# Three attention stages of an fp32 transformer kernel rewritten: dilated attention by query classes over 688 keys, weighted sums turned round

## The reference

```python
def neighbourhood_attention(q, k, v, rpb):      # each query: 8 rows x 16 columns of keys
    s = q.k * d ** -0.5 + bias;  pr = softmax(where(valid, s, NEG));  return pr @ v

DIL_CONFIGS = ((128, 1), (512, 4), (2048, 16))  # (window, dilation)
def dilated_branch(q, k, v, pos, slopes, window, dil):
    # query t attends to t + j*dil for |j| <= window // (2*dil)
    s = q.k * Dh ** -0.5 - slopes * abs(pos_q - pos_k)
    ...
def dilated_attention(...):                     # the three branches, weighted by their denominators
    return sum(outs * softmax(lses))

def latent_attention(...):                      # MLA: q and k of width 96 (64 + 32 rotated)
    s = (qn.kn + qr.kr) * scale;  p = softmax(s);  return p @ v
```

## Time and profile before

| what | value |
|---|---|
| median of 3 runs | 4692.28 us (4685.75 to 4693.0) |
| profiled execution, its own time | 4690.71 us |
| span of the profile | 4688.9 us |
| PE busy | 4082.2 us, 87% of the span |
| DVE, ACT, POOL busy | 48%, 32%, 37% |
| mean granted clock of PE | 0.948 of full speed |

### The profile page before, as it was taken

One profiled execution on the slowest core, in us unless ns is written; L12 is line 12 of the kernel. 1 busy time (PEld: TensorE's weight loads), 2 busy tenths in 40 slices (PEclk: granted clock), 3 DMA queues, 4 the chain that ended last, 5 costly groups with the idle time before them and its releaser, 6 DMA issues.

```text
span 4688.9 us, 60744 instructions
## 1 busy us (share of the span) xinstructions
PE 4082.2 (87%) x22152; PEld 3480.2 (74%) x22152; DVE 2228.0 (48%) x4269; ACT 1503.3 (32%) x2417; POOL 1736.7 (37%) x1140
## 2 busy tenths in 40 slices
PE   3999575788789798998899999688898996999998
PEld 2788465776577687886688888576887885888887
DVE  2443585532366565553444443465565544323323
ACT  2221243431233674441221211232773432222221
POOL 2432123531255462002544444353560003544442
PEclk9999888999899899998999999899999998999999
DMA  6765332631135422212223221245322221111111
GB/s 152 207 179 149 98 89 64 138 100 50 72 88 140 111 60 66 48 50 90 78 84 108 77 99 32 76 119 146 84 55 63 54 80 49 50 49 54 45 45 50
DMA packets 300704, 404.65 MB, mean 86 GB/s; under 512 B 45908, under 2 KB 224980, under 8 KB 299860
## 3 DMA queue, kind: packets, MB, share of 16 engines
q1 hardware_dynamic: 293496, 375.60, 28.5%
q10 hardware_dynamic: 6912, 25.17, 1.8%
HBM read 316.23 MB, written 93.63 MB: 87 GB/s over the span
## 4 chain that ended last, share of the span: by engine, by line
PE 68%; issue 8%; DVE 7%; POOL 5%; DMA 3%; SPq 2%; DVEq 2%; ACT 2%; POOLq 1%; ACTq 0%
PE ps L881 10%; PE ps L456 6%; PE ps L458 5%; PE ps L457 5%; PE ps L871 5%; PE ps L1834 5%; PE ps L1835 5%; PE ps L1836 5%; PE ps L1850 5%; PE ps L1852 4%; PE ps L1851 4%; POOL rs L770 2%; PE ps L917 1%; DVEq L1235 1%; PE ps L1507 1%
## 5 line engine op out<-in xcount | busy, mean ns | idle before, releaser
L405 POOL TENSOR_TENSOR WL<-RAW,WH 128x1024 fp32r<-128x1024 f32 x226 | 556.6, 2476 | 1195.1 <-ACT WH L387 1184.9
L456 PE MATMUL ps<-WH,XTh 128*128 128x512 f32 (+1 forms) x1536 | 616.9, 402 | 70.6 <-issue 34.8
L457 PE MATMUL ps<-WH,XTl 128*128 128x512 f32 (+1 forms) x1536 | 604.2, 393 | 0.0
L458 PE MATMUL ps<-WL,XTh 128*128 128x512 f32 (+1 forms) x1536 | 604.0, 393 | 0.0
L387 ACT ACTIVATE WH<-RAW 128x1024 fp32r<-128x1024 f32 x226 | 234.1, 1057 | 794.2 <-PE ps L1852 347.8
L1870 DVE TENSOR_TENSOR X<-ps,X 128x512 f32<-128x512 f32 x512 | 349.0, 689 | 254.1 <-PE ps L1852 253.1
L1850 PE MATMUL ps<-WH,Hh 128*128 128x512 f32 x1024 | 401.3, 392 | 4.3 <-DVE X L1870 4.0
L1834 PE MATMUL ps<-XTh,WH 128*128 128x512 f32 x1024 | 400.4, 391 | 1.2 <-issue 1.2
L1835 PE MATMUL ps<-XTl,WH 128*128 128x512 f32 x1024 | 398.9, 390 | 0.0
L1836 PE MATMUL ps<-XTh,WL 128*128 128x512 f32 x1024 | 398.8, 389 | 0.0
L1852 PE MATMUL ps<-WL,Hh 128*128 128x512 f32 x1024 | 398.6, 389 | 0.0
(11 more groups left out here) (196 smaller groups left out, 7664.0 us busy)
## 6 DMA issues: line engine op xcount, KB each, us to landing
RAW<-w_all SPq DMA_DIRECT2D x232, 512.0 KB, 4.0
WM<-w_mod ACTq DMA_DIRECT2D x48, 512.0 KB, 4.2
WM<-w_mod SPq DMA_DIRECT2D x48, 512.0 KB, 4.0
QS<-QA_d SPq DMA_DIRECT2D x24, 512.0 KB, 3.9
KHs<-KA_d SPq DMA_DIRECT2D x48, 256.0 KB, 6.0
KLs<-KA_d SPq DMA_DIRECT2D x48, 256.0 KB, 6.5
VS<-VA_d SPq DMA_DIRECT2D x20, 512.0 KB, 7.3
X<-x SPq DMA_DIRECT2D x2, 4096.0 KB, 12.8
```

The source lines that it names most:

```text
L405: e.tensor_tensor(w_low(n), w_raw(n), w_high(n).bitcast(F32), ALU.subtract).then_inc(w_ready, 1)
L456: e.matmul(bank, a, w, start=(kc == 0), stop=False)
L457: e.matmul(bank, b, w, start=False, stop=False)
L458: j = e.matmul(bank, a, l, start=False, stop=(kc == K - 1))
```

## The change

In all three stages the sum over the keys is turned round: the values are split into a high and a low fp32r part that stand side by side (64 + 64 columns, VHL) as the stationary operand, and the turned probabilities, also split into high (PTh, ACT) and low (PTl, DVE), are the moving one with 512 queries, for four units (a group G) at once. The 128 x 512 result is copied by ACT to OT, and PE turns it back and adds the two halves by four plain fp32 matmuls of 64 columns against twoI (two identities on top of each other). DVE divides and writes four tiles of Y at once. The negation of the maximum is folded in. The two halves of 4 heads are one run of 64 units.

Dilated attention takes as a unit not 128 neighbouring queries but one residue class mod 4 of 512 queries. Its keys are then 576 near ones and 112 far ones of the same class, 688 in place of 1024. A query's slope is folded into q (POOL multiplies the eps and sums of squares of a head by a table column, `by_head`), so that the bias ND is a table that stays and gets one addition of log counts per head. The output product's transposes put Y's dilated columns back in order of tokens (`by_class`, a write with a stride of 4).

NA and dilated attention ("narrow") share one body, `band_pe`, `band_act`, `band_dve`, and MLA has `heads_pe` and so on. In the narrow body the scores run two units ahead, probabilities have three buffers, the first four turned pieces go to bank 4 + u % 2 and the rest (one in NA, two in dilated) to bank 7, which is a single buffer; bank 6 holds the sum.

```diff
+        def band_pe(who, a):
+            def scores(u):
+                at = band(a, u)
...
+                if u >= 2:
+                    e.wait_ge(s["max"], a.u0 + min(u - 1, N_UNITS))
...
+                G = hosts_back(u)
+                if G is not None:
+                    e.wait_ge(s["ot_copied"], a.g0 + G + 1)
+                    for r in range(4):
+                        c = at.back + 64 * r
+                        j = e.matmul(flat(2 * (u % 2), c, c + 64), a.OT[:, G % 2, r * P:r * P + P], twoI[:], start=True, stop=True)
+                    j.then_inc(s["back"], 1)
...
+                for keys, c in at.keys:
+                    to = flat(2 * (u % 2), c, c + len(range(S)[keys]))
+                    e.matmul(to, Q[:, h % 2, at.queries], KH[:, h % 2, keys], start=True, stop=False)
+                    j = e.matmul(to, Q[:, h % 2, at.queries], KL[:, h % 2, keys], start=False, stop=True)
+                j.then_inc(s["full"], 1)
+            def turn_first(u):
+                e.wait_ge(s["exp"], a.u0 + u + 1)
+                ge(e, s["lo"], 2 * (a.u0 + u) - 3)
...
+            def turn_rest(u):
+                at = band(a, u)
+                ge(e, s["lo"], 2 * (a.u0 + u))
+                for src, c in at.rest:
+                    j = e.transpose(ps[0:src.stop - src.start, 7, c:c + P], Pt[:, u % 3, src], ident[:])
+                j.then_inc(s["tr"], 1)
...
+            scores(0)
+            scores(1)
+            for u in range(N_UNITS + 6):
+                G, r = divmod(u - 1, 4)
+                if u < N_UNITS:
+                    turn_first(u)
+                    turn_rest(u)
+                scores(u + 2)
+                if 1 <= G <= N_GROUPS and r < 3:
+                    values(G - 1, r)
...
+        def band_dve(who, a):
...
+            maxes(0)
+            for u in range(N_UNITS + 7):
+                if u + 1 < N_UNITS:
+                    maxes(u + 1)
+                if 1 <= u <= N_UNITS:
+                    low(u - 1)
+                if u % 4 == 2 and u >= 10:
+                    output(u // 4 - 2)
...
+        def heads_pe(who, a):
...
+            scores(0)
+            for u in range(N_UNITS + 4):
+                G, r = divmod(u, 4)
+                if u + 1 < N_UNITS:
+                    scores(u + 1)
+                if u < N_UNITS:
+                    turn(u)
+                if G >= 1 and r < 3:
+                    values(G - 1, r)
+                if G >= 1 and r == 3:
+                    turn_back(G - 1)
```

More of the change, by code:

```diff
@@ L814, in in_cell, with qk_kind @@
             return lambda kc: (first + kc // kper, (kc % kper) * width)
-        def qk_kind(dst, gain, first):
+        def qk_kind(dst, gain, first, by_head=False):
             def store(e, t, m, slot):
@@ new lines, in build_program, with __init__ @@
+        class Dilated:
+            def __init__(self, u):
+                g, c = divmod(u % T, 4)
+                self.g, self.first, self.width = g, 0, DIL_KEYS
+                self.queries = slice(512 * g + c, 512 * g + 512, 4)
+                if g == 0:
+                    far = slice(576 + c, S, 4)
+                    self.flat, self.nat, self.back = 0, 0, 768
+                    self.keys = [(slice(0, 512), 0), (slice(512, 576), 512), (far, 576)]
+                    self.rest = [(slice(512, 512 + DIL_FAR), 0), (slice(576, DIL_KEYS), P)]
+                    self.rest_rows = DIL_FAR
+                else:
+                    far = slice(c, 448, 4)
+                    self.flat, self.nat, self.back = S - DIL_KEYS, DIL_KEYS - 512, 512 - 512
+                    self.keys = [(far, 336), (slice(448, 512), 448), (slice(512, S), 512)]
+                    self.rest = [(slice(48, 48 + P), 0), (slice(0, P), P)]
+                    self.rest_rows = P
@@ new lines, in na_pool @@
+        def na_pool(who, a):
+            e, s = who.e, a.s
+            value_low(e, a, 0)
+            for u in range(N_UNITS):
+                h, t = divmod(u, T)
+                if t == 0:
+                    e.wait_ge(*a.loaded(h))
+                    nab = NAB[:, h % 2, :].rearrange("p (a b) -> p a b", b=GRID_W)
+                    e.tensor_tensor(nab, nab, rows3(CMK[:], NA_E, GRID_W), ALU.add)
+                    e.drain()
+                if u >= 3:
+                    e.wait_ge(s["max"], a.u0 + u - 2)
+                e0 = (NA_START[t] - 2 * t + 8) * GRID_W
+                e.tensor_tensor(BIn[:, u % 3, :], NAB[:, h % 2, e0:e0 + NA_KEYS], RMK[:, NA_KIND[t], :], ALU.add).then_inc(s["bias"], 1)
+                if u % T == 7 and u + 1 < N_UNITS:
+                    value_low(e, a, u // T + 1)
@@ new lines, in dil_attention @@
+                    g, c = divmod(t, 4)
+                    if g == 0:
+                        parts = [(slice(0, 576), slice(0, 576)), (slice(576, DIL_KEYS), slice(576 + c, S, 4))]
+                    else:
+                        parts = [(slice(0, DIL_FAR), slice(c, 448, 4)), (slice(DIL_FAR, DIL_KEYS), slice(448, S))]
+                    for cols, keys in parts:
+                        j = e.activation(ND[:, t, cols], POSF[:, keys], ACT.Abs, bias=rs1[:, t:t + 1])
+                    j.then_inc(s["dist"], 1)
@@ L1976, in layout @@
     out["pos_cols"] = v["positions_2"][0].reshape(T, P).T
+    out["pos_class"] = v["positions_2"][0].reshape(2, P, 4).transpose(1, 0, 2).reshape(P, T)
     out["w_mod"] = v["w_mod_2"]
```

719 lines of the change are left out of this document (458 added, 261 removed).

## The result

The changed kernel takes 4753.93 us (median of 4 runs, 4752.26 to 4755.9) against 4689.01 us for the kernel before (4 runs, 4684.69 to 4693.0): the ratio is 1.0139, 95% interval 1.0121 to 1.0156. The forecast was 4660, range 4605 to 4735: wrong in sign and outside the range. The profiled execution took 4752.26 us, its span 4750.4, 61.5 more than before.

The account below looks back on a forecast made before the run. PE was taken to bound dilated attention and MLA before, a loop of waits the narrow stages after; +23 (NA) + 0 (dilated) - 62 (MLA) + 3 (elsewhere) + 6 (clock) = -30 gave 4660 us, range 4605 to 4735.

Parts of the forecast that it names:

- The loop of waits: Narrow units: turned rest, scores, maximum and both low parts follow each other without overlap, once a unit.
- its sum: Loop terms added up: 3.80 us a dilated unit (3.73 before) and 3.33 us an NA unit.
- I take 0.107: PE, new small fp32r products: 0.107 us each, since each has one weight load; bounds 0.03 to 0.06 and 0.214.
- the second rival: Small products at plain fp32 pace, or slow strided reads: 0.43 us a dilated unit, 0.21 an NA unit; 4728 us; chance 0.15.
- one sentence: Query weights and keys read with stride 4: no row shows whether they cost more; the high bound covers it.
- I put 6 us for a few such stretches: Narrow stages: a few stretches at half clock, where the loop grows by 1.1 us, cost 6 us in all.
- the third rival: Narrow stages: clock falls to 0.88, half clock a quarter of the time, 0.28 us a unit; 4707 us; chance 0.14.
- PE's share of work: Argument against a falling clock: PE works 65 to 70% of the loop, a little above differential attention.
- the start and the tail of the stage: Dilated attention: first counted maximum about 3.5 us later than the old first one, tail 11 us; stage 246 us, no difference.
- NA: the number: NA stage 23 us slower: first maximum 6 us later, 210 us of units, tail 10.5, against 203 before.
- MLA: MLA units 3.50 us, 0.56 less, with a longer tail: 31 us gained a layer, 62 in all.
- Elsewhere: Other stages: `by_head` costs 3 us; strided writes by ACT and DVE nothing, at most 10.

Follow-up runs that it names:

- Experiment 2: Changed kernel with PE's turned rest moved behind the scores of unit u+2: 4540.22 us, ratio 0.9679 to the kernel before.
- Experiment 8: Changed kernel with contiguous dilated queries (other than the reference's) and three no-work products between PE's two turned parts: 4644.16 us, ratio 0.9904 to the kernel before.
- experiment 1: Changed kernel with dilated queries from 128 contiguous columns, so other queries than the reference's: 4696.6 us, ratio 1.0017 to the kernel before.
- experiment 4: Changed kernel with a filler, three small no-work products between PE's two turned parts in narrow units: 4722.1 us, ratio 1.0067 to the kernel before.
- experiment 7: Changed kernel with turned rest behind the scores and GpSimd copying each head's queries sorted by class: 4475.96 us, ratio 0.9546 to the kernel before.
- experiment 5: Changed kernel with turned rest behind the scores and contiguous dilated queries (other than the reference's): 4475.32 us, ratio 0.9546 to the kernel before.

## Why the prediction was wrong

- **The loop of waits: right in place and members, its sum partly by luck.** In the changed kernel DVE waited 322.5 us for PE's scores before its 128 dilated maxima, and PE waited before L1418 for DVE's low part (0.73 us in the row at 1707.98). Experiment 2 opens the loop by moving one of its members. Experiment 8's averages, 3.82 us (3.80) and 3.30 us (3.33), look like its sum measured, but each has a term too much and one too little. Dilated: turned rest 0.17 (0.21) and scores to maximum 1.19 to 1.22 (1.30) make a round of 3.66, and the filler and the start of the stage fill it up to 3.82. NA: turned rest to maximum is 1.00 (0.11 + 1.12), a unit without turn-backs 2.90 (3.12), and seven changes of head of 4.6 to 5.5 us, at which the sum had put nothing, bring the average back up.
- **"I take 0.107" for the small products: this term failed, in dilated attention.** It was right where queries are contiguous (0.11 in experiment 1, and in the changed kernel's own value products). Loads with a stride of 4 fp32 numbers follow each other after 0.22 to 0.23 us. It was the second rival, 0.15 with slow strided reads in it, whose price of 0.43 us a unit came out at 0.46 (experiment 1 against the changed kernel) and, at nearly full clock, 0.60 (experiment 4 against 8, 277.92 - 240.35 = 37.6 us for 63 units); its NA part did not come, as NA's queries have no stride. A row of before could not show it, and I let one sentence stand for a cost that the change adds to all six score products of a unit. The Trainium skill (SBUF — State Buffer, section Door 1: The DMA port swizzle) has the rule that I left out: SBUF is read in lines of 16 bytes, and an access that goes to a new line each time pays. A stride of 4 fp32 numbers is just 16 bytes. The trace agrees, 0.19 us for a contiguous load and 0.33 for a strided one. No run here has another stride, so it is not shown here that the line of 16 bytes is the reason.
- **"I put 6 us for a few such stretches" of lower clock: mis-sized.** It was the third rival in dilated attention: a granted clock of 0.76, lower than the 0.88 of differential attention that I took for the rival. Its price, 1.1 us a unit times 0.48, would be 0.53. The windows give 0.25 (experiment 4 against the changed kernel) to 0.39 (experiment 8 against 1); with the filler's own 0.50 us in every fourth unit taken out, 0.37 to 0.52. So the price was about right, and what failed was the choice of 6 us in its place. I had gone by PE's share of work, and this case's rows do not bear that out: PE was busy for 249 of 294 us in the dilated window at a clock of 0.76, for 164 of 214 in NA at 0.86, and for 83 of 120 in differential attention before at 0.88. What sets the clock stays open; the runs show that it rose when the pauses were filled (experiment 4) and when the loop was opened (experiment 2).
- **The two together** are 293.90 - 240.35 = 53.6 us from first to last maximum in layer 0 and 48.7 in layer 1, 102 of the 123 us of both layers. The other 10 us a layer lie in the start and the tail of the stage: in the changed kernel the first two units took 9.6 us, forecast 3.5, and 15.2 us lie behind the last maximum, forecast 11 (layer 0).
- **NA: the number right, in part by luck,** +25.0 against +23. The first maximum came 0.6 us later and not 6; the 63 units took 214.2 us against 210, with the low clock in them (experiment 4 gives 4.9 us less), and the tail 13.2 against 10.5.
- **MLA: right in mechanism, too small.** 3.38 us a unit ((2130.46 - 1917.46) / 63) against 3.50, and before 4.10 ((2086.64 - 1828.43) / 63) against the 4.06 of the one unit that I had read, since the average holds the pause between the two halves. After the change the four units of a group repeat as 3.66, 3.66, 3.17 and 3.16 us, each some 0.1 under its forecast. The stage ran at full clock and PE was busy for 220 of 225 us. Two layers gave 85 us instead of 62.
- **Elsewhere: nothing clear.** The stretches between the stages differ by -2.9 to +3.7 us each, -1.3 in all, and the first of them, ahead of NA, differs by as much between runs that do not touch it (+3.7 here, -0.5 in experiment 7). No run takes `by_head` or the strided writes by ACT and DVE by themselves.

So two rivals, held at 0.15 and 0.14 and priced one by one, came true together. 68 and 47 (53 for the 6 in the sum) on top of 4660 make 4775; less the NA part of the first, 13, and the 23 that MLA gave more, 4739, against 4754 measured. The starts and tails of the dilated stages, 20 us beyond the forecast, are not in this sum; the units of the loop, 0.14 us below theirs, work against them.

## What to carry to other kernels

Two in-order engines that each place a wait ahead of work that the other needs make a loop that no buffer shows: write down one round of it, and move the member that is free to move before anything else; here one line was worth 214 us, and the clock of the dilated stages came back by itself. An average that agrees with a sum proves little until its single units are looked at, and a probe such as the filler has a cost of its own. An order that opens one loop may close another through a third engine (low parts first), so list the whole round for each order. When a change lets an operand be read with a new stride, price that load from the nearest row and the stride in bytes, and think of a sorted copy by an engine that has time. Once a loop is open, look at the seams it covered, such as the change of head here.

## What was not expected of the hardware

- A weight load of 128 x 128 with a stride of 16 bytes takes 0.31 to 0.33 us and follows the one before after 0.22 to 0.23, against 0.19 and 0.11 for a contiguous one. It sets the pace of products of 64 and 112 columns, and even between the two 512-column products of a unit it shows: 0.43 us from the first to the second (1708.18 to 1708.61 in the changed kernel) against 0.31 (1701.90 to 1702.21 in experiment 1).
- The strided read by GpSimd (1135 ns for 512 columns) costs nothing that the whole shows: experiment 7 takes 4475.96 us, experiment 5 without the copy 4475.32.
- Two pauses of PE in four dilated units, one of 0.7 and one of 1.7 us in some 18 us, with PE busy for 85% of the window, went with a granted clock of 0.76, where the same work with fillers in the pauses had 0.95.
- A DVE operation with two SBUF operands can stand behind GpSimd. In experiment 7, at a change of head:

```profile
903.18 2.64 POOL L1595 TENSOR_TENSOR NAB<-NAB,CMK 128x1152 f32<-128x1152 f32 x1 [0.18 <-issue]
...
903.89 2.21 DVE L1563 TENSOR_TENSOR Y<-TMPn,ZSn 128x256 f32<-128x256 f32 x1
```

The same operation took 0.43 us at 894.68; here it ends 0.28 us behind GpSimd's operation. The Trainium skill (SBUF — State Buffer, section SBUF: two separate sides) says that the two share a pair of ports that one holds for a whole instruction; this row agrees.

Left open: bank 7 has room for two slots of 256 columns, which by the order of waits would open the loop without a new order. That was not tried, so no run shows it.
